# Attention and gating stage: value tile last of the projections, its turn within the heads, Gelus ahead of them, other places for sums and scalings

## What is computed

```python
h = rms_norm(x, attn_norm_g)
q, k, v, u, vv = split(h @ w_in)            # 512, 128, 128, 512, 512 columns
q, k = axial_rope(rms_norm(q)), axial_rope(rms_norm(k))
attn_o = gqa_attention(q, k, v)             # 8 heads of 64, 2 heads of keys and values
vv = rms_norm(gelu(vv), by heads)           # 8 heads of 64
mixed = sg_w[h] @ vv + sg_b                 # within chunks of 128 tokens
sg_o = gelu(u) * mixed
x = x + concat(rms_norm(attn_o), rms_norm(sg_o)) @ w_o
```

## Time and profile before

| | us |
|---|---|
| median of 3 runs | 2478.93 |
| lowest and highest | 2478.63, 2483.83 |
| the profiled execution | 2477.12 |
| its span, first to last instruction | 2475.3 |
| TensorE busy | 2393.8 (97% of the span) |
| VectorE, ScalarE, POOL busy | 1473.9, 1077.8, 160.6 |

### The profile page before, as it was taken

The page is one execution under the profiler, slowest core; times in us unless marked ns, Lnnn a source line. Parts: engine busy times, 40 slices in busy tenths (PEclk is TensorE's granted clock), DMA queues, the critical chain, the costliest instruction groups (busy, mean ns, idle before and its releaser), DMA issues.

```text
span 2475.3 us, 33356 instructions
## 1 busy us (share of the span) xinstructions
PE 2393.8 (97%) x11723; PEld 1947.7 (79%) x11723; DVE 1473.9 (60%) x2142; ACT 1077.8 (44%) x1458; POOL 160.6 (6%) x159
## 2 busy tenths in 40 slices
PE   8999999999899989999999899999999989999998
PEld 6766788888788878888887677888888767788887
DVE  7886554532677636554226766887533686687732
ACT  5346433332456644333324543554423473454421
POOL 2011100000100011000002021000011011000000
PEclk9999999999999999999999999999999999999999
DMA  7331233333222222333333102333334202233331
GB/s 173 68 94 51 74 105 94 91 94 103 69 74 71 76 68 77 101 94 97 94 99 94 57 1 77 110 100 96 91 96 120 72 12 60 82 105 93 98 93 64
DMA packets 400952, 209.69 MB, mean 85 GB/s; under 512 B 18131, under 2 KB 397655, under 8 KB 400871
## 3 DMA queue, kind: packets, MB, share of 16 engines
q1 hardware_dynamic: 397111, 199.65, 27.9%
q0 software_dynamic: 3424, 8.91, 1.4%
q10 hardware_dynamic: 336, 0.05, 0.0%
HBM read 204.38 MB, written 4.19 MB: 84 GB/s over the span
## 4 chain that ended last, share of the span: by engine, by line
PE 86%; DVE 8%; ACT 3%; issue 2%; DVEq 1%; DMA 0%; ACTq 0%; SPq 0%
PE bank L677 69%; PE bank L723 4%; PE bank L727 2%; DVE w_lo L1907 2%; PE bank L1288 1%; ACT w_hi L1364 1%; DVEq L1936 1%; PE bank L1264 1%; DVE small L2690 1%; DVE tmp L1939 1%; PE bank L1239 1%; PE bank L1160 0%; PE bank L1202 0%; PE bank L753 0%; PE bank L1118 0%
## 5 line engine op out<-in xcount | busy, mean ns | idle before, releaser
L1907 DVE TENSOR_TENSOR w_lo<-w_raw,w_hi 128x1024 fp32r<-128x1024 f32 x380 | 475.4, 1251 | 614.9 <-ACT w_hi L1364 609.7
L677 PE MATMUL bank<-h_hi,w_hi 128*128 128x512 f32 x1840 | 728.0, 396 | 10.4 <-DVEq L1936 9.1
L677 PE MATMUL bank<-h_lo,w_hi 128*128 128x512 f32 x1840 | 718.0, 390 | 0.0
L677 PE MATMUL bank<-h_hi,w_lo 128*128 128x512 f32 x1840 | 717.7, 390 | 0.0
L1364 ACT ACTIVATE w_hi<-w_raw 128x1024 fp32r<-128x1024 f32 x380 | 401.6, 1058 | 664.6 <-PE bank L677 647.4
L677 PEld LDWEIGHTS bank<-h_hi,w_hi 128*128 128x128 f32 x1840 | 346.5, 188 | 86.6 <-issue 7.8
L677 PEld LDWEIGHTS bank<-h_hi,w_lo 128*128 128x128 f32 x1840 | 346.5, 188 | 72.8 <-issue 2.7
L677 PEld LDWEIGHTS bank<-h_lo,w_hi 128*128 128x128 f32 x1840 | 346.0, 188 | 72.9
L677 PE MATMUL bank<-hid_lo,w_hi 128*128 128x512 f32 x704 | 274.1, 389 | 0.0
L677 PE MATMUL bank<-hid_hi,w_lo 128*128 128x512 f32 x704 | 274.1, 389 | 0.0
L677 PE MATMUL bank<-hid_hi,w_hi 128*128 128x512 f32 x704 | 274.1, 389 | 0.0
(11 more groups left out here) (466 smaller groups left out, 2857.9 us busy)
## 6 DMA issues: line engine op xcount, KB each, us to landing
w_raw<-in_ffn_w SPq DMA_DIRECT2D x120, 512.0 KB, 3.8
w_raw<-in_w_up SPq DMA_DIRECT2D x88, 512.0 KB, 3.7
w_raw<-in_c_w_in SPq DMA_DIRECT2D x32, 512.0 KB, 4.0
w_raw<-in_w_down SPq DMA_DIRECT2D x32, 512.0 KB, 3.7
w_raw<-in_w_in SPq DMA_DIRECT2D x28, 512.0 KB, 3.9
w_raw<-in_w_o SPq DMA_DIRECT2D x16, 512.0 KB, 3.6
w_raw<-in_ab_w_in SPq DMA_DIRECT2D x12, 512.0 KB, 6.4
w_raw<-in_ffn_w SPq DMA_DIRECT2D x16, 384.0 KB, 3.2
```

The lines of the kernel that those rows point to most:

```text
L677: mm = nc.tensor.matmul(out[:], w[:, s, k], v[:, kt], start=(kt == 0 and w is w_hi and v is hi), stop=(kt == sum(slabs) - 1 and v is lo))
L1907: nc.vector.tensor_tensor(w_lo[:, s], w_raw[:, s], w_hi[:, s].bitcast(F32), ALU.subtract).then_inc(lo_done, 1)
```

## The change

It moves the value tile (5) to the end of `IN_ORDER`, so that the last Gelu (tile 9) is made before the heads and `LAST_GELU_AT` goes. The sums of squares come after six tiles instead of seven. TensorE's value turn moves behind unit 1 of the heads, the gating weights' turn behind the tenth tile instead of the ninth, and ScalarE's copies and its square root for the gating one place in the order later. On VectorE the first three maxima come before the gating's reciprocal and scalings, which are dealt out over the first units; the weight split of the last tile moves to unit 16; `shares` moves one unit earlier and ahead of the gating work. The diff, cut to its core:

```diff
@@ -30,7 +30,6 @@
 SHARE_AT = (12, 20, 28)
-LAST_GELU_AT = 4
 SCORE_BANKS = ((2, 3, 4), (0, 1, 4))
@@ -38,7 +37,7 @@
 
-IN_ORDER = [4, 5, 0, 1, 2, 3, 10, 11, 12, 13, 6, 7, 8, 9]
+IN_ORDER = [4, 0, 1, 2, 3, 10, 11, 12, 13, 6, 7, 8, 9, 5]
 RING = 4
@@ -382,7 +381,6 @@
             sem(k) for k in ("score_ready", "max_ready", "exp_ready", "prob_turned", "head_done"))
-        last_gelu = sem("last_gelu")
         copied_by_scalar, copied_by_vector = sem("prob_copied_by_scalar"), sem("prob_copied_by_vector")
@@ -1143,7 +1141,7 @@
                 enter(*((tmp[:, (KD - 1) % 4], 0) if i else (sq_in[:, KD - 1], 8)))
-                product(h_hi, h_lo, [KD], 3)
+                product(h_hi, h_lo, [KD], 2)
                 out = take(4)
@@ -1175,17 +1173,13 @@
                 nc.tensor.matmul(out[:], swap, qa[:, 4], start=True, stop=True).then_inc(k_swapped, 1)
-                out = take(5)
-                pe.wait_ge(v_in, n(v_in))
-                for t in range(TT):
-                    mm = nc.tensor.transpose(out[:, t * P:(t + 1) * P], va[:, t * P:(t + 1) * P], ident)
-                mm.then_inc(v_turned, 1)
+                product(h_hi, h_lo, [KD], 2)
                 for v in range(2):
...
                     mm.then_inc(sgw_turned, 1)
-                product(h_hi, h_lo, [KD], 2)
+                product(h_hi, h_lo, [KD], 1)
                 pe.wait_ge(vv_in, n(vv_in))
@@ -1230,6 +1224,8 @@
                     out = take(b) if (t, keys[0]) == (0, 0) else bank[b]
+                    if (j, t, keys[0]) == (0, 0, 0):
+                        pe.wait_ge(v_copied, n(v_copied))
                     if keys[0] == 0:
@@ -1241,6 +1237,14 @@
 
+                def turn_values():
+
+                    out = take(5)
+                    pe.wait_ge(v_in, n(v_in))
+                    for t in range(TT):
+                        mm = nc.tensor.transpose(out[:, t * P:(t + 1) * P], va[:, t * P:(t + 1) * P], ident)
+                    mm.then_inc(v_turned, 1)
+
                 def spread_share(j):
@@ -1253,7 +1257,6 @@
                 pe.wait_ge(q_turned, n(q_turned))
-                pe.wait_ge(v_copied, n(v_copied))
                 for u in range(LOOK):
@@ -1265,6 +1268,8 @@
                         scores(u + LOOK)
+                    if u == 1:
+                        turn_values()
 
@@ -1724,7 +1729,7 @@
                 for t in IN_ORDER:
-                    if t == IN_ORDER[6]:
+                    if t == IN_ORDER[5]:
                         act.wait_ge(qk_summed, n(qk_summed))
@@ -1740,9 +1745,6 @@
                             act.drain().then_inc(qk_in, 1)
-                    elif t == 5:
-                        nc.scalar.activation(va[:], bank[b][:], ACT.Copy).then_inc(bank_free[b], 1)
-                        act.drain().then_inc(v_in, 1)
                     else:
@@ -1753,21 +1755,19 @@
                         act.drain().then_inc(vv_in, 1)
-                        act.wait_ge(v_turned, n(v_turned))
-                        nc.scalar.activation(v_tok[:].rearrange("p t w -> p (t w)"), bank[5][:], ACT.Copy).then_inc(bank_free[5], 1)
-                        act.drain().then_inc(v_copied, 1)
+                    if t == 6:
                         for v in range(2):
...
                         act.drain().then_inc(sgw_copied, 1)
-                    if t == 6:
+                    if t == 7:
                         for v in range(TT):
...
                         act.drain().then_inc(vv_copied, 1)
-                    if t == 8:
+                    if t == 9:
                         act.wait_ge(vv_summed, n(vv_summed))
@@ -1799,15 +1799,16 @@
                     h, t = u // TT, u % TT
-                    if u == LAST_GELU_AT:
-                        act.wait_ge(bank_scaled, n(bank_scaled))
-                        nc.scalar.activation(ua[:, 3], ua[:, 3], ACT.Gelu_apprx_tanh).then_inc(last_gelu, 1)
                     if u not in BY_VECTOR:
...
                         act.drain().then_inc(copied_by_scalar, 1)
+                    if u == 1:
+                        act.wait_ge(v_turned, n(v_turned))
+                        nc.scalar.activation(v_tok[:].rearrange("p t w -> p (t w)"), bank[5][:], ACT.Copy).then_inc(bank_free[5], 1)
+                        act.drain().then_inc(v_copied, 1)
                     if u - 3 in MIX_AT:
@@ -2666,23 +2667,27 @@
                 scaled_tile()
-                dve.wait_ge(vv_rooted, n(vv_rooted))
-                settle()
-                step(nc.vector.reciprocal(gate_dev, gate_dev))
-                settle()
-                for t in range(TT):
+                def gate_inverse():
+
+                    dve.wait_ge(vv_rooted, n(vv_rooted))
+                    settle()
+                    step(nc.vector.reciprocal(gate_dev, gate_dev))
+
+                def gate_normal(t):
+
+                    settle()
                     tt(vv_tok[:, t].rearrange("p (h d) -> p h d", h=8), vv_tok[:, t].rearrange("p (h d) -> p h d", h=8),
                        gate_dev[:, 8 * t:8 * t + 8].unsqueeze(2).to_broadcast([P, 8, HEAD]), ALU.mult)
-                flag(vv_normal)
+                    if t == TT - 1:
+                        flag(vv_normal)
 
...
                     b = at["bank"] % RING
-                    own(nc.vector.tensor_tensor(ua[:, 3], bank[b][:], inv_all, ALU.mult), bank_scaled)
+                    own(nc.vector.tensor_tensor(va[:], bank[b][:], inv_all, ALU.mult), v_in)
                     flag(bank_free[b])
                     at["bank"] += 1
-                    split()
 
@@ -2729,6 +2734,8 @@
                     maxima(u)
+                gate_inverse()
+                gate_normal(0)
                 last_tile()
@@ -2739,6 +2746,12 @@
                         maxima(u + LOOK)
+                    if u + 1 < TT:
+                        gate_normal(u + 1)
+                    if u == MIX_AT[-1] + 6:
+                        split()
+                    if u + 2 in SHARE_AT:
+                        shares(SHARE_AT.index(u + 2))
                     if u - 1 in MIX_AT:
@@ -2746,13 +2759,9 @@
                         flag(bank_free[5])
-                        if j == 3:
-                            dve.wait_ge(last_gelu, n(last_gelu))
                         own(nc.vector.tensor_tensor(ua[:, j], ua[:, j], mixed[:], ALU.mult), gated_ready)
...
                         gated_low(MIX_AT.index(u - 5))
-                    if u + 1 in SHARE_AT:
-                        shares(SHARE_AT.index(u + 1))
                     if u - 1 in SHARE_AT:
```

## The result

The changed kernel takes 2489.72 us (median of 8 runs) against 2483.27 for the kernel before (8 runs, taken beside them): ratio 1.0040, 95% interval 1.0029 to 1.0051. The 1.0040 is 9.9 us, slower by 0.4%, where I had forecast no change (+3.7 us) with a lean to slower; it's the size of my slower rival (+9.7). One execution of the kernel of the second experiment took 4029.31 us and is in no ratio. The profiled execution took 2487.51 us, its span is 2485.7.

A forecast was written before the change was run, and what follows sets the result against it. TensorE, busy nearly throughout, bounds the kernel. Projections lose 4.3 us a stage, heads gain 3.5, leaving 0.84; with 1.0 for the clock, 2 x (0.84 + 1.0) = +3.7, so 2482.6 us by the median, range 2476.5 to 2490.

The forecast's parts named there:

- my slower rival: The clock falls in both new TensorE waits, 2.0 us each: +9.7 us, 2488.6 in all; chance 0.28.
- (a): Projections: with the value turn moved, no wait at the gating weights' turn; gain 2.96 us a stage.
- (b): Fourth and fifth rotation matmul: new waits near 2.6 and 1.4 us, released by VectorE; loss 4.1 a stage.
- (c): Swap behind the eighth tile: new wait near 3.1 us for VectorE's scaling of k; loss 3.2 a stage.
- (d): Start of the heads: no first wait, seventh unit's turn 10.5 us after the last tile, before 13.2; gain 2.7.
- (e): Spreading of the shares in the heads: TensorE's wait of 1.69 us falls to some 0.25; gain 1.4.
- (f): VectorE's backlog in the heads: wait for a copied bank at unit 17 grows from 0.82 to 1.6 us; loss 0.6.
- (g): TensorE's clock at the new waits: 1.7 us at (b) with chance six in ten, so 1.0; nothing at (c).
- My bounds: Clock loss at the two new TensorE waits: each 0 to 2.3 us, together 0 to 4.6 a stage.
- my own signs of being wrong: Prediction wrong if (b) and (c) are absent, heads win over 5 us a stage, or clock falls twice more in each.

The follow-up runs named there:

- the second experiment: The changed kernel with VectorE's scaling of the seventh and all later tiles one place later, sums still after six tiles: 2471.16 us, ratio 0.9951.
- the first experiment: The changed kernel with the sums of squares after seven tiles again, all else as in the change: 2467.41 us against 2479.96, ratio 0.9943.
- its two variants: The kernel before with shares one unit earlier alone, ratio 0.9988, and with the first maxima ahead of the gating scalings alone, ratio 1.0010.

## Why the prediction was right or wrong

- (a) Value turn and weights' turn: right. There is no wait at L1180; the weights' turn follows its tile, and with the other waits gone the 2.96 are in the gain of the first experiment.
- (b) The wait at the rotation matmuls: right. Forecast 2.6 and 1.4, the eighth tile 6.4 after the seventh's end; the trace has 2.64 and, in the second stage, where it stands apart, 0.72; it is shorter than forecast in part because the fourth matmul, for which I had counted 0.7 us of work, shows 1.31, partly at the half clock. The tile comes 6.8 after the seventh's end (1359.37 - 1352.60); with the clock up (11, 5 and 13 small matmuls) it is 6.25 (1359.24 - 1352.99).
- (c) The wait at the swap: right, 3.1 forecast, 3.10 measured, the swap starting at 1370.11.
- (d) The start of the heads: right, 10.5 forecast, 10.7 measured. I had named both reasons without a share for each: by the experiments 1.8 of the 2.5 hang on the Gelu's leaving, 0.7 on the maxima's order, and the order is worth nothing while the Gelu is there.
- (e), (f): 0.25 forecast at the spread, 0.48 measured; 1.6 at unit 17, 1.25 measured. The heads gained 3.25 in all, 3.5 forecast.
- (g) **The step that failed.** I took 1.0 a stage for the clock: a fall worth 1.7 behind (b) with a chance of six in ten, and none behind (c), "whose wait is nearer to the 2.36". Both came, in both stages, and cost 3.5 by the trace of the change and 3.6 and 4.35 by the kernel with small matmuls in the waits. From the end of the seventh tile to the swap that kernel is 2.1 us faster in the first stage and 2.7 in the second, which is the price of (b); the rest, 1.5 and 1.7, is that of (c), for which I had put nothing. At (b) the fall lasted 6.8 us, twice the 3.4 at the sums from which I had the 1.7; at (c) it lasted 3.4. My reason for nothing at (c) was one wait of 2.36 without a fall, and the runs show how little that says: a wait of 2.39 at the same place, in the kernel with rotations between the sums, had a fall in one stage and none in the other. Without the clock, 2 x (4.3 - 3.25) = 2.2 of the 9.3 remain.

With the right size the sum is 2 x (0.84 + 3.5) = +8.7, against 9.3 between the marks. It was the slower rival, in its mechanism and its places; its price of 2.0 for each wait (4.0 a stage) was near the 3.6 and 4.35, its chance of 0.28 too small. My bounds had it in: 0 to 4.6. One of my own signs of being wrong, the clock falling twice more in each stage, is what the trace shows. That 2489.72 us still lies inside my range of 2476.5 to 2490 is no merit of the forecast: the range reached up to that rival, and the median of the kernel before was 4.3 us higher in the new measurement than in the one I started from.

## What to carry to other kernels

When one engine's program is moved by a step and its partner's isn't, write the two orders side by side and look for an item that now stands ahead of its cause; here one tile of slack was the whole cover, and with it kept the same change gains 0.6%. Cost a new wait of some 3 us on TensorE with a fall of its clock, not as a chance but as the likely case: here the falls added 3.6 to 4.35 us a stage to the waits' 7. Move work within a chain only with the bound of that chain: the maxima's order was worth nothing beside the Gelu, and 0.7 us a stage without it.

## What the runs showed of the hardware that I hadn't expected

- A wait of 3.10 us on TensorE came with 3.4 us at the 1.2 GHz level in both stages, and a wait of 2.64 with one of 0.7 to 0.9 close behind with 6.8 us in four of four stages (the change, and the swap behind the ninth tile). A wait of 2.8 in the heads came with 6.8 us in one stage and none in the other. Waits of 2.36 to 2.39 at the gating weights' turn came with a fall of 3.4 us in one stage of eight: none in the kernel before and its two variants, one in two with the rotations between the sums. So the length of a wait alone doesn't decide in this range.
- The length of the fall at the sums of squares varies at the same work: in the kernel with sums after seven tiles it was 3.4 us in the first stage and 6.8 in the second, in both of its profiled executions, and its two stages differ by 1.2 us with it. With the sums between rotations it was 0 and 0, then 0 and 10.2 with VectorE's order changed.
- Whether the clock falls at a place also varies between executions of one program. Of those same two executions one has falls of 3.4 us at about 205 and 636 us, far ahead of the stage, and the other has none there; its first mark stands at 1319.64 instead of 1316.53. The executions of the kernel before group in a like way: most take 2477 to 2480 us at a mean granted clock of 0.992 to 0.994, a second group about 2482 to 2484 at 0.991, a third 2485 to 2486 at 0.990. A step of some 3 us would be two more falls of 3.4 us, like the 3.1 between those two executions; that is an estimate, as no slower execution of that kernel was profiled. Of the changed kernel's eight executions three took 2492.6 to 2495.9 us at 0.986 to 0.987, the other five 2487.5 to 2489.9 at 0.989; the profiled one is of the five.
- A small identity matmul of 128 columns in full float32 is two records in the trace and takes 0.227 us of TensorE's time, the pair.
